# A DeltaNet encoder kernel: the short convolution's middle tap goes to ScalarE, and the scaling of the input rows is placed later

## What is computed

```python
h = x @ w_in
qkv, z, b, a = jnp.split(h, ...)
qkv = jax.nn.silu(_short_conv(qkv, conv_w))     # 5 taps along the tokens, one weight per channel and tap
q, k, v = jnp.split(qkv, [DN_K_DIM, 2 * DN_K_DIM], axis=-1)
...                                              # gated delta rule, both directions, chunks
x = _layernorm(DEEPNORM_ALPHA * x + y, ln1_g[i], ln1_b[i])
```

## Time and profile before

| what | value |
| --- | --- |
| median of 3 runs | 1866.23 us (1861.76 to 1868.33) |
| the profiled execution | 1864.28 us, its span 1862.5 us |
| PE busy | 1580.2 us, 85% of the span |
| DVE busy | 878.0 us, 47% |
| ACT busy | 326.6 us, 18% |
| POOL busy | 159.3 us, 9% |
| mean granted TensorE clock | 0.922 of full speed |

### The profile page before, as it was taken

How to read it: one execution, slowest core, us unless ns; L and a number is a source line. 1 busy time by engine, 2 the same in 40 slices (tenths; PEclk the granted TensorE clock), 3 DMA queues, 4 the chain that set the end, 5 groups by cost and what they waited for, 6 DMA issues and landing times. The chain is left out here.

```text
span 1862.5 us, 20168 instructions
## 1 busy us (share of the span) xinstructions
PE 1580.2 (85%) x6814; PEld 990.2 (53%) x6814; DVE 878.0 (47%) x1786; ACT 326.6 (18%) x737; POOL 159.3 (9%) x143
## 2 busy tenths in 40 slices
PE   7894999999999999999887399973899997389990
PEld 4473576585765857658585244432555553334440
DVE  3562564665656656566564311116145456311115
ACT  2120122121221212212121011101222221011110
POOL 1200200202002020020200100002000000100002
PEclk9997999999999999999996599996899998599995
DMA  5782110101101011000104489945021112669964
GB/s 184 221 270 76 45 45 23 45 23 45 45 23 45 23 45 45 23 23 0 46 1 153 167 270 354 352 157 175 0 81 36 46 34 73 235 208 351 355 233 144
DMA packets 150500, 219.69 MB, mean 118 GB/s; under 512 B 8584, under 2 KB 120448, under 8 KB 150464
## 3 DMA queue, kind: packets, MB, share of 16 engines
q1 hardware_dynamic: 138464, 176.50, 29.6%
q10 hardware_dynamic: 7392, 25.96, 4.0%
q0 software_dynamic: 4608, 16.78, 2.5%
HBM read 175.70 MB, written 43.52 MB: 118 GB/s over the span
## 5 line engine op out<-in xcount | busy, mean ns | idle before, releaser
L1395 PE MATMUL bank<-moe_wgu,moe_xgT 128*96 128x512 f32 x512 | 228.0, 598 | 1.5 <-DVE moe_xgT L1602 1.5
L404 PE MATMUL bank<-xT,wqkv 128*128 128x512 f32 x448 | 211.0, 601 | 9.6 <-DVE conv L896 9.6
L1395 PEld LDWEIGHTS bank<-moe_wgu,moe_xgT 128*96 128x96 f32 x512 | 81.9, 165 | 123.2 <-issue 123.2
L1602 DVE COPY moe_xgT<-bank 128x384 f32<-128x384 f32 x34 | 19.0, 558 | 226.5 <-PE bank L1386 226.5
L488 PE MATMUL bank<-wz,xT 128*128 128x256 f32 x512 | 118.3, 381 | 0.9 <-DVE res L1089 0.9
L404 PEld LDWEIGHTS bank<-xT,wqkv 128*128 128x128 f32 x448 | 78.1, 191 | 74.3 <-issue 63.6
L1412 PE MATMUL bank<-moe_wd,moe_hidT 128*96 128x512 f32 x256 | 115.2, 593 | 1.8 <-DVE moe_hidT L1610 1.8
L620 PE MATMUL bank<-wo,oT 128*128 128x512 f32 x256 | 115.7, 602 | 0.8 <-ACT oT L772 0.8
L488 PEld LDWEIGHTS bank<-wz,xT 128*128 128x128 f32 x512 | 96.3, 191 | 14.2 <-issue 1.7
L896 DVE SCALAR_TENSOR_TENSOR conv<-bank,taps,conv 128x510 f32<-128x510 f32 (+1 forms) x128 | 95.2, 744 | 0.6
L987 DVE TENSOR_TENSOR TU<-TU,bank 128x512 f32<-128x512 f32 x112 | 75.7, 686 | 16.2 <-PE bank L547 7.3
(11 more groups left out here) (297 smaller groups left out, 2445.1 us busy)
## 6 DMA issues: line engine op xcount, KB each, us to landing
moe_wgu<-moe_w_gate SPq DMA_DIRECT2D x32, 1024.0 KB, 10.5
moe_wgu<-moe_w_up SPq DMA_DIRECT2D x32, 1024.0 KB, 13.0
moe_wd<-moe_w_down SPq DMA_DIRECT2D x32, 1024.0 KB, 6.2
wqkv<-dn_w_in SPq DMA_DIRECT2D x32, 512.0 KB, 4.0
moe_x_rows<-slots_x ACTq DMA_DIRECT2D x34, 384.0 KB, 7.3
slots_y<-moe_y_rows ACTq DMA_DIRECT2D x32, 384.0 KB, 6.0
slots_x<-o SPq DMA_DIRECT2D x1, 9984.0 KB, 51.2
slots_y<-o SPq DMA_DIRECT2D x1, 9984.0 KB, 92.6
```

The source lines that it names most:

```text
L404: mm = pe.matmul(bank[:], wqkv[:, ct, k], xT[:, k], start=k == 0, stop=k == KD - 1)
L1395: mm = pe.matmul(ps[2][0:CAP], xgT[:, r, k], wgu[:, r, k].rearrange("p a f -> p (a f)"), start=k == 0, stop=k == KD - 1)
```

## The change

ScalarE multiplies the bank by the middle tap's weight and writes `conv`, in a new step `middle_tap`, and VectorE adds the four other taps, the first of them behind a wait for ScalarE (`tap_ready`). This holds for the groups prepared inside the loop; the convolutions of head 0 ahead of the loop keep all five taps on VectorE. In the table of slots each group now has four jobs in place of five, and the `silu` of groups 1, 2 and 3 stands one slot earlier. Ahead of the loop the scaling of `res` moves behind the convolution of group 1 and the silu of group 0.

```diff
+            def middle_tap(uses, i, ct):
+
+                bank = got(uses, f"proj{ct}", i)
+                act.wait_ge(taps_ready, i + 2)
+                act.wait_ge(kqT_ready, i * 2 + 2)
+                act.mul(conv[:, ct], bank[:], taps[:, ct, 2:3]).then_inc(tap_ready, 1)
...
                 if with_next:
+                    middle_tap(uses, i, 0)
+                    middle_tap(uses, i, 1)
                     act_silu(i + 1, 0)
...
+                    if with_next and l in (3, 5):
+                        middle_tap(uses, i, 2 + l // 5)
                     if with_next and l in (3, 4):
                         act_silu(i + 1, l - 2)
...
-            for tt in range(TT):
-                dve.wait_ge(xT_ready, 2 * tt + 2)
-                step(nc.vector.tensor_scalar(res[:, tt], res[:, tt], ALPHA, None, ALU.mult))
-
...
                     bank = got(uses, f"proj{ct}", i)
-                    if ct >= 2:
-                        dve.wait_ge(v_ready, i * 2 + ct - 1)
                 w = taps[:, ct]
-                if 2 in taps_of:
+                if 2 in taps_of and not first:
+                    dve.wait_ge(tap_ready, i * 4 + ct + 1)
+                elif first:
                     dve.wait_ge(taps_ready, n + 1)
                     step(nc.vector.tensor_scalar(conv[:, ct], bank[:], w[:, 2:3], None, ALU.mult))
...
                     silu(0, ct - 1)
+                if ct == 1:
+                    for tt in range(TT):
+                        dve.wait_ge(xT_ready, 2 * tt + 2)
+                        step(nc.vector.tensor_scalar(res[:, tt], res[:, tt], ALPHA, None, ALU.mult))
...
-                        todo = [lambda ct=ct, j=j: convolve(uses, i, i + 1, ct, taps_of=(j,)) for j in (2, 0, 1, 3, 4)]
+                        todo = [lambda ct=ct, j=j: convolve(uses, i, i + 1, ct, taps_of=(2, 0) if j == 0 else (j,)) for j in (0, 1, 3, 4)]
                         for k, job in enumerate(todo):
                             jobs.setdefault(min((0, 5, 11, 17)[ct] + k, 23), []).append(job)
-                        jobs.setdefault((8, 13, 18, 23)[ct], []).append(lambda ct=ct: silu(i + 1, ct))
+                        jobs.setdefault((8, 12, 17, 22)[ct], []).append(lambda ct=ct: silu(i + 1, ct))
```

More of the change, by code:

```diff
@@ L230, in delta_net @@
         osq_ready, oss_ready, og_ready, oT_ready, y_ready = (sem(n) for n in ("osq_ready", "oss_ready", "og_ready", "oT_ready", "y_ready"))
+        tap_ready = sem("tap_ready")
         zeroed, zero_filled = sem("zeroed"), sem("zero_filled")
@@ L1107, in _ @@
             body(NK - 1, LAST, False, per)
-DN_DVE_STEPS = 4 * 4 + 2
+DN_DVE_STEPS = 4 * 3 + 2
 class Steps:
```

## The result

The changed kernel takes 1838.07 us (median of 6 runs, 1829.51 to 1840.52) against 1866.23 (1861.76 to 1870.19). The ratio is 0.984, 95% interval 0.9821 to 0.9859: faster by 1.6%, or 29.9 us of 1866.23, and from 26 to 33 by the interval.

A forecast was written before the change was run, and what follows sets the result against it. The zero fill was taken to set head 0's scan, and TensorE's waits to bound heads 1 to 6. Loop 9.3, earlier fill 6.0 and clock 6.8 us sum to 22.1, giving 1844.1 us, range 1838 to 1855.

The forecast's parts named there:

- The loop: Heads 1 to 6: two shortened TensorE waits, 1.55 us a head, 9.3 us in all, bounds 8.2 to 10.1.
- The fill sets head 0, and moves with its issue: Ahead of the loop: moving the scaling issues the zero fill earlier and head 0's scan follows, 6.0 us, bounds 4.4 to 6.4.
- Part 1: Ahead of `proj2` in the loop: group 0's last tap comes one slot earlier, TensorE's whole wait goes, 1.37 us a head.
- Part 2: Levels 5 and 6: silu moved out, first tap waits for ScalarE; level-6 mask 0.18 us earlier a head, bounds 0 to 0.3.
- the chain: VectorE from group 3's first tap to the mask of level 6: 4.95 us, where it was 5.84.
- Part 4: Behind the output's turn, heads 1 to 6: four of six clock falls of 1.69 us go, 6.8 us, bounds 0 and 10.1.
- its rule: Skill's rule that multiplies belong on VectorE, up to three times faster; if it held, the loop would give nothing.
- the falls did not stay: Rival: clock falls stay in all six heads because the idle time before them is untouched, 1850.9 us; chance 0.24.
- the fill's end did follow its issue: Rival: the zero fill's end doesn't follow its issue, 1850.1 us, or 1856.9 if clock falls stay too; chance 0.10.
- the handoffs did not eat the gain: Rival: late first tap keeps the wait ahead of `proj2`; about 1860.2 us, or 1853 with clock falls gone; chance 0.06.
- nothing waited for ScalarE's copies: Slower case: group 3's late `middle_tap` delays ScalarE's level-6 copies, the matmuls and the scan, 1872 us; chance 0.02.

The follow-up runs named there:

- The scaling alone: Kernel before with only the four scalings of the residual rows moved behind the convolution of group 1: ratio 0.9974, median 1859.45 against 1864.45 us.
- the three other kernels: Changed kernel with VectorE making the middle tap (1838.38 us), or with two (1855.52 us) or one (1846.35 us) extra matmuls per head that prepares another.
- the fill from `oT`: Changed kernel with the zero fill read from tile `oT` and its wait moved to ScalarE: ratio 0.9688, median 1807.71 us.
- The added matmuls: Extra 512-column matmuls per head that prepares another: changed kernel with two 0.9927, with one 0.9889; kernel before with two 1.0002.

## Why the prediction was right in its steps and wrong in their sizes

The step that failed is the size of two terms. The loop was put at 9.3 us, 10.1 at most, and gave 11.8: above all the term for levels 5 and 6, 0.18 us a head, which measured 0.40. And the term for the clock counted four of six falls, 6.8 us, where five or six went, 8.5 to 10.1.


- **The fill sets head 0, and moves with its issue**: right. The issue came 6.56 us earlier, forecast 6.0, with 6.4 as the upper bound. I had added up modelled ends; the starts give 58.28 - 51.85 = 6.43. The four scalings took 2.87 us in place of 5.05 and cost nothing in their new place, as said. The scaling alone measured 4.9 (2.8 to 6.9). The scan of head 0, forecast at 157.7, starts at 157.4, 157.7 and 158.2 in the profiles of the three other kernels that have the new loop and the early issue and read the fill from `o`.
- **Part 1, the last tap of group 0**: the mechanism is right, and the term was mis-sized: 1.37 from the row, 1.54 by the starts of the two matmuls.
- **Part 2, levels 5 and 6**: the handoff (0.72 against 0.73 us) and the chain (4.93 against 4.95) came out, 5.84 - 0.72 - 4.93 = 0.19 us. The term lacked the 0.21 us between the two masks of level 6. I had read only the first of TensorE's two stops there, and counted the instructions of the last level and not which of them is followed by a wait for itself. I forecast the first stop at 0.7 to 0.8 us, and it stayed at 0.91; the second, 0.32 us, went. Its upper bound, 0.3, was too narrow by the same omission. A head without a fall was forecast at 112.9 us and is 112.47.
- **Part 4, the clock**: the other term that fell short. I took four of six falls to go and kept 0 and 10.1 as bounds; none of the six was left in the profile. In the other profiles with the shorter heads none of heads 1 to 6 (the fill from `oT`, which has one in head 0 instead) or only head 6 (the two others) was left with it, so five or six went. That is 8.5 to 10.1 us against 6.8. The added matmuls showed the cause that I had only argued: what decides is where in time the idle stretch comes, and the distance of the heads repeats that place or moves it.
- **The sum**: with the measured terms it is 6.5 for the issue, 6 x (116.12 - 1.69 - 112.47) = 11.8 for the loop, and 8.5 to 10.1 for the clock, 26.8 to 28.4, in the interval of 26 to 33. The forecast had 22.1. The range's lower end was built from bounds that were too tight for the loop (10.1 where 11.8 was measured) and for the issue, and the result fell there. How many falls are left is read from one profile of each kernel.
- **What I didn't doubt and should have**: that ScalarE's part was what the change lives by. I priced its handoff and its rule with care, and found the slot's wait on TensorE, but didn't ask what the same slots would do with the tap left on VectorE. The trace had it: 1.03 us of waiting ahead of the tap of level 5, and 0.88 in each block step.

The rivals: the falls did not stay; the fill's end did follow its issue; the handoffs did not eat the gain; nothing waited for ScalarE's copies.

What stays open: why the fill took 86.8 us in one execution and 91 to 93 in the others, and what part of the difference between the medians' gain (28.2) and the ratio's (29.9) is such scatter.

## What to carry to other kernels

When work is moved to another engine, separate the place that it frees from the work: a table of slots that ends a group one step earlier can be the whole gain, and leaving the work where it was is the test. In a loop of nearly equal rounds, a fall of TensorE's clock can repeat in every round or in none (here in six of six heads before, in none after), so compare the distance of rounds with and without it before a few us are put down to an edit. And read for what a buffer is held: a DMA that reads 4 KB per partition for 90 us held the one tile that the scan needed, and another tile gave back 30 us.

## What the runs showed of the hardware that I had not expected

- Extra work on TensorE can be free: 1.72 us in each of seven heads, six of them on the path, left the time of the kernel before at 1.0002 (0.9982 to 1.0022), since six falls of 1.69 us went.
- Four scalings of 128x1024 on VectorE took 2.87 us, 0.69 each, where GpSimd had nothing to do, and 5.05 beside it; GpSimd's four instructions took 4.07 us instead of 5.95. The Trainium skill (SBUF — State Buffer, the section SBUF: two separate sides) says that the two engines share a pair of ports, and that an instruction of GpSimd and one of VectorE of certain kinds exclude each other on it for the whole instruction. The trace agrees that they hold each other up: side by side a scaling takes 1.42 us against 0.69. It doesn't show whole turns: the pairs follow each other every 1.45 us, where one after the other they would take 0.69 + 4.07 / 4 = 1.71.
